# Unread identity products on TensorE ahead of eleven waits of a two-block transformer kernel

## What is computed

```
x = first_block(x, c, ctx, c_ctx, ...)    # attention layer, then a Hyena long-convolution layer, then rms_norm
x = second_block(x, c_2, ...)             # even layer: conv + stick-breaking attention, then a mixture of experts
                                          # odd layer: gated linear recurrence, then a mixture of experts
# every layer: h = rms_norm(x) * (1 + scale) + shift ; x = x + gate * mixer(h)
# shift, scale, gate = silu(c) @ mod_w + mod_b
# attention layer: 8 grouped-query heads and 8 latent heads over 256 context + 1024 own tokens
# experts: 16 experts, 4 groups, two experts for each token, silu(x@w1) * (x@w3) @ w2
```

## Time and profile before

| | us |
|---|---|
| median of 3 runs | 4669.76 |
| lowest and highest | 4667.46 and 4686.14 |
| the profiled execution's own time | 4669.6 |
| span of the profile (first to last instruction) | 4667.8 |

### The profile page before, as it was taken

One profiled execution on the slowest core, in us unless ns is written; L12 is line 12 of the kernel. 1 busy time (PEld: TensorE's weight loads), 2 busy tenths in 40 slices (PEclk: granted clock), 3 DMA queues, 4 the chain that ended last, 5 costly groups with the idle time before them and its releaser, 6 DMA issues. The chain is left out here.

```text
span 4667.8 us, 76042 instructions
## 1 busy us (share of the span) xinstructions
PE 4083.4 (87%) x28639; PEld 2076.3 (44%) x28639; DVE 2024.0 (43%) x3133; ACT 1044.1 (22%) x2136; POOL 266.1 (6%) x382
## 2 busy tenths in 40 slices
PE   4799799998999998999599978868999599949995
PEld 1445366564444446878344435432333244413331
DVE  1233588773222207999447737441111334321112
ACT  0122355441111112222020336211010244100000
POOL 0100000000000000111100000000000200000001
PEclk7899799999999989999799989989999799969997
DMA  8122433334445410111520030246963611376767
GB/s 329 29 71 66 97 77 86 79 84 170 173 183 221 147 64 12 55 56 55 181 95 26 38 118 28 91 154 259 362 261 126 194 36 50 104 312 250 273 232 269
DMA packets 254230, 643.61 MB, mean 138 GB/s; under 512 B 53434, under 2 KB 132372, under 8 KB 218176
## 3 DMA queue, kind: packets, MB, share of 16 engines
q1 hardware_dynamic: 218312, 524.26, 32.2%
q0 software_dynamic: 19424, 94.01, 5.6%
q10 hardware_dynamic: 16280, 22.27, 1.3%
HBM read 1325.95 MB, written 113.53 MB: 308 GB/s over the span
## 5 line engine op out<-in xcount | busy, mean ns | idle before, releaser
L1085 PE MATMUL att_acc<-att_kT,att_qT 96*128 96x512 f32 (+3 forms) x768 | 305.9, 583 | 35.9 <-DMA att_kT<-scratch_KT 19.7
L1741 PE MATMUL hyp_acc<-hy_hT,hyp_early_weights 128*128 128x512 f32 x768 | 335.9, 596 | 0.0
L3641 PE MATMUL blocks_h<-moe_w,blocks_xT 128*32 128x512 f32 x2560 | 294.2, 612 | 19.0 <-DMA moe_w<-in_ex_w 19.0
L3641 PE MATMUL blocks_h<-od_hT,blocks_xT 128*32 128x512 f32 x1280 | 288.2, 604 | 21.3 <-DMA moe_w1b<-in_ex_w 16.2
L3641 PE MATMUL blocks_h<-moe_w1b,blocks_xT 128*32 128x512 f32 x1280 | 288.2, 604 | 0.0
L3663 PE MATMUL blocks_acc<-moe_w,blocks_hidT 128*32 128x512 f32 x2560 | 284.6, 597 | 3.4 <-DMA moe_w<-in_ex_w 2.1
L1004 DVE TENSOR_REDUCE att_part_max<-att_acc 128x1 f32<-128x512 f32 (+1 forms) x384 | 214.6, 586 | 98.3 <-PE att_acc L1085 98.3
L2396 PE MATMUL evp_acc<-ev_hT,evp_early_weights 128*128 128x512 f32 x512 | 225.7, 602 | 7.6 <-DVE evp_qkT L2537 5.6
L1741 PEld LDWEIGHTS hyp_acc<-hy_hT,hyp_early_weights 128*128 128x128 f32 x768 | 145.2, 192 | 174.1 <-issue 174.0
L1085 PEld LDWEIGHTS att_acc<-att_kT,att_qT 64*128 64x128 f32 (+1 forms) x768 | 130.0, 198 | 127.3 <-issue 82.9
L3641 PEld LDWEIGHTS blocks_h<-od_hT,blocks_xT 128*32 128x32 f32 x1280 | 76.7, 112 | 216.1 <-issue 212.2
(11 more groups left out here) (555 smaller groups left out, 6528.9 us busy)
## 6 DMA issues: line engine op xcount, KB each, us to landing
moe_w<-in_ex_w SPq DMA_DIRECT2D x640, 1024.0 KB
od_hT<-in_ex_w SPq DMA_DIRECT2D x168, 1024.0 KB
moe_w1b<-in_ex_w SPq DMA_DIRECT2D x168, 1024.0 KB
hyp_m_weights<-in_mod_w POOLq DMA_DIRECT2D x6, 8192.0 KB, 24.9
mod_weights<-in_ada_w SPq DMA_DIRECT2D x12, 2048.0 KB, 20.7
att_v<-scratch_V SPq DMA_DIRECT2D x64, 320.0 KB, 5.7
scratch_y_rows<-blocks_x ACTq DMA_DIRECT2D x40, 512.0 KB, 7.7
hyp_early_weights<-in_hy_w_in SPq DMA_DIRECT2D x8, 2048.0 KB, 27.2
```

What stands on the lines that cost most here:

```text
L1085: nc.tensor.matmul(scores(j, c), qT[e, s, cols], kT[e, s, CHUNKS[c]], start=True, stop=True).then_inc(scored[c], 1)
L1741: mm = nc.tensor.matmul(acc[:, m % 2, half * NC:(half + 1) * NC], weights[:, ws, kt, c:c + P], hT[:, kt, half * NC:(half + 1) * NC], start ...
L3641: mm = nc.tensor.matmul(out[mine, :], xT[:, kt, mine], w[l][:, kt, :], start=(kt == 0), stop=(kt == KT - 1))
```

## The change

`keep_busy` issues `4 * us` matmuls that multiply the identity with itself, start and stop set, into a part of PSUM which the stage's first real product overwrites. They stand in TensorE's list ahead of a wait. No semaphore is raised or waited for by them. `stage_modulations` gets `ident` as a new argument. Nothing is removed, and no other engine's list changes.

```diff
+def keep_busy(nc, out, ident, us):
+    for _ in range(4 * us):
+        nc.tensor.matmul(out, ident[:, 0:out.shape[0]], ident[:, 0:out.shape[1]], start=True, stop=True)
...
# stage_modulations
+                keep_busy(nc, acc[:, 0, 0:P], ident, 10)
                 pe.wait_ge(svec_ready, signals(1))
# attention_project (ctx and lat)
+                keep_busy(nc, acc[:, 0, 0:P], ident, 5)
                 pe.wait_ge(cols_in, signals(16 * 3))
# stage_attention
+                keep_busy(nc, acc[:, 0:P], ident, 14)
                 pe.wait_ge(stacked, signals(1))
# project_out (ao, ho and eo), first in TensorE's list
+                keep_busy(nc, acc[:, 0, 0:P], ident, 8)
# stage_stick_breaking
+                keep_busy(nc, scores[:, 0, 0:P], ident, 9)
                 pe.wait_ge(barred_ready, signals(1))
# stage_recurrence
+                keep_busy(nc, px[:, 0, 0:P], ident, 6)
                 blocks(pe, front, back)
# moe_blocks (twice), first in TensorE's list
+                keep_busy(nc, acc[:, 0, 0:P], ident, 8)
                 pe.wait_ge(tables_in, signals(16 * 3))
...
                 nc.tensor.matmul(owner_row, owner_col, ident[:, 0:PLACES], start=True, stop=True).then_inc(owner_turned, 1)
+                keep_busy(nc, acc[:, 0, 0:P], ident, 6)
                 pe.wait_ge(located, signals(1))
...
                 def first():
+                    keep_busy(nc, acc[:, 0, 0:P], ident, 7)
                     rows(0, 0)
# moe_combine, with a norm
+                    keep_busy(nc, h_turn[:, 0, 0, :], ident, 5)
                     pe.wait_ge(cols_in, signals(16 * 3))
                     nc.tensor.transpose(col_turn[:, :], col_rows[:, :], ident[0:3 * KT, 0:3 * KT]).then_inc(cols_turned, 1)
+                    keep_busy(nc, h_turn[:, 0, 0, :], ident, 9)
                     for t in range(TT):
```

More of the change, by code:

```diff
@@ L209, in load_rows, with stage_modulations @@
         sp.dma_start(early.col_rows[n * KT:(n + 1) * KT, :], v.rearrange("(kt p) -> kt p", p=P)).then_inc(early.cols_in, 16)
-def stage_modulations(nc, d, svec, early):
+def stage_modulations(nc, d, ident, svec, early):
     S, Q = 2, MODS_AT_ONCE
@@ L3972, in program @@
             early = Projection(nc, outer)
-            stage_modulations(nc, d, svec, early)
+            stage_modulations(nc, d, ident, svec, early)
             stage_attention_project(nc, d, ident, early)
```

## The result

| | before | after |
|---|---|---|
| median of 12 runs, us | 4670.68 | 4691.57 |
| lowest and highest | 4664.37, 4686.14 | 4686.49, 4699.32 |
| ratio, 95% interval | | 1.0046, 1.0038 to 1.0054 |
| span of the profile | 4667.8 | 4691.6 |

The change makes the kernel 20.9 us slower, 0.46%. The forecast was 4676, +6 us; the time lies in the range given, near its upper end. So the sign was right and 15 of the 21 us were missing.

The account below looks back on a forecast made before the run. TensorE was taken to bound most stages, with gains only in dense work at the low clock just behind a wait. The places' terms summed to +6.1 us on 4669.6, about 4676, range 4656 to 4694.

Parts of the forecast that it names:

- `project_out`: Stages `ao`, `ho`, `eo`: 32 products each overshoot their room; net +0.7, 0 and +1.6 us.
- Prices: Every fill: a product takes 0.22 us at the high clock, 0.44 at the low one.
- The low part of a fill: Start of every fill: the clock stays low for 3 to 6 us, taken as 4, before it rises.
- the first rival: All fills: identity products don't raise the clock, each lasts 0.44 us; about +80 us, 4750; 7 in 100.
- rivals 1 and 2: All fills: products don't raise the clock (4750, 7 in 100), or cost 0.38 us each (4700, 5 in 100).
- Attention: Attention: 56 products overshoot by 7.5 us, faster first scores return part, the raised clock is soon lost; net +3 us.
- The third rival: Clock holds through the attention's scores and gaps in `ctx`, `lat`, `ao`: 4662, or 4650; 8 in 100.
- `lat`: Stage `lat`: room 2.8 us, fill 6.4, part returned by faster transposes and projection; net +2 us, bounds +1 and +3.6.
- `ctx`: Stage `ctx`: room 2.0 us, fill 6.4, 3.4 returned by the high clock; net +1 us, bounds -0.7 and +4.4.
- recurrence: Recurrence: fill overshoots by 0.4 us, the 32 passes behind it regain 1.6; net -1.2 us, bounds -1.5 and +1.
- Stick-breaking: Stick-breaking attention: overshoot 4.2 us, hidden by values arriving late and faster scores; 0, bounds -0.5 and +3 us.
- The rule: Whole kernel: penalty is throttled length times one minus granted share, 327 us; the prediction held only 27 us at most buyable.

Follow-up runs that it names:

- e7: The kernel before with 112 added products in the attention alone, instead of 56: 4699.43 us, ratio 1.0068 to before.
- e4: The kernel before with the change's 56 products in the attention alone: 4674.42 us, ratio 1.0010 to before.
- e6: The kernel before with 20 products ahead of the attention's first wait and 4 behind the scores of each of its first four tiles: 4660.12 us.
- e9: The kernel before with e6's attention products, 12 in `eo` behind the two increments and 24 in the recurrence: 4660.16 us, ratio 0.9978.
- e5: The kernel before with 20 products in the attention, 12 in `eo` behind the two increments, 24 in the recurrence, none elsewhere: 4663.79 us.
- e1: The changed kernel with the 32 products in `project_out` moved behind TensorE's two increments: 4679.28 us, ratio 1.0021 to before.
- the third pair: Two executions of e10, attention 2.0 us apart: 4663.99 us (median of its runs) and 4665.98 us (the single second execution).
- e10: The kernel before with 4 products behind the scores of each of the attention's first four tiles, no fill ahead: 4663.99 us, ratio 0.9987.

## Why the prediction was right, and where it was not

The time lies in the range because the range was 38 us wide, and the place that made most of the loss was priced at almost nothing. That the time came out inside is in part luck. The mechanism was right for the products themselves and wrong for what stood behind them in `project_out`.

**Prices: right.** A product was put at 0.22 us; e7 against e4 gives 0.2225. The low part of a fill was put at 3 to 6 us: 5.6 in the attention, and the fills' durations fit (7.25 for 20 products forecast at 6.4, 9.28 for 32 at 9.0, 7.04 for 24 at 7.3, 15.44 and 14.52 for 56 at 14.3). Identity products raise the clock, so the first rival was wrong. The row held against it was weaker than the prediction made of it: the 16 transposes at `eo` last 3.87 us and the clock was low for 6.0, so matmuls filled the rest. The 0.12 for slower is rivals 1 and 2 alone, with nothing in it for a tail of the forecast.

**Attention: right mechanism, size within its bounds.** Start at the block's start, clock low and then high, first eight scores in 2.84 us, clock lost in the first tiles: all as written. +3 was forecast, 3.8 and 5.0 us were measured by adding and removing the fill. The third rival's clock that holds by itself didn't come; e6, e9 and e5 show how far filled gaps help.

**`lat`: right; `ctx` and recurrence: not to be told from chance.** `lat` +1 to +2.7 for +2, with L633 now released by TensorE. `ctx` came out at -2.1 to +0.2 for the +1, but a kernel without products there had -2.4. The recurrence's 32 passes took 13.90 us for the 14 forecast; the stage itself lay between -2.4 and +2.5 for the -1.2.

**`project_out`: the step that failed.** The prediction costed the products there as an overshoot only: "an overshoot of this size ends in the 7.33 us in which TensorE waited" (`ho`), "the third tile's gate product waits for a transfer until 1085.37 in any case" (`ao`). Both took the arrival of the transfers as fixed. They aren't: the list of TensorE begins with two increments that release the sync queue's loads, and the products stood ahead of them. The later gates moved with the loads, in `ao` the third one by 11.0 us (from 1085.37 to 1096.34) against a stage start that was 5.3 later. Forecast +0.7, 0 and +1.6; measured +5.7, +3.6 and +3.6. With the increments first (e1) the same products cost -0.2, +0.1 and +2.9, a sum of 2.8 for the forecast 2.3: close as a sum, with `ao` 0.9 us below and `eo` 1.3 above their terms, for the code that I had in mind, and wrong for the code in the diff. The place ahead of a queue's release was 12.3 of the missing 15 us.

**Stick-breaking: under-sized.** 0 was forecast with +3 as the upper bound, -0.2 or +3.4 came. Of the 3.4 in the changed kernel 1.3 are there 17 us behind the block's start, the rest comes later, with the low stretches; whether the products in `ho` place these is open. The long convolution's +3.7 in the profiled run is chance and belongs to no step. Expert stages and combine moved by 1 to 2 us in both directions, within their bounds.

**The rule.** The prediction weighed the Trainium skill's penalty, TensorE: Matmul & The Clock Gate, section Terms, against what stands directly behind a release. The runs bear the second out: 118 us of low clock fewer would be an estimated 59 us by that rule, and the kernel became slower. It does fit two pairs of executions in the attention's later tiles (10.6 us more at the low clock, 5.4 us longer; 7.5 and 4.0), and not the third pair.

## What to carry to other kernels

Before anything is put at the head of an engine's list, look what stands behind it that others wait for, increments above all: they take no time in the profile and can release a whole stage's transfers. Size filling work by the time from the block's start to the release, not by the idle time shown, and let it end just short of it: 12 products behind the increments earned 3.0 us where 32 behind them cost 2.9 and 32 ahead of them 3.6. Where a raised clock is lost again in a stretch short of work, a few passes in its gaps (1.2 us per tile in the attention) were worth more than a long fill ahead of it (4660.12 in e6 against 4674.42 in e4).

## What the runs showed of the hardware

- The two increments behind 64 passes took effect ahead of the passes' end: SP issued 1.9 us before the fill's end, as the profile models it, in all three stages (1071.19 against 1073.11 in `ao`). So TensorE's instruction stream runs ahead of its array there.
- Whether passes over 64 rows keep a raised clock depends on what stands between them: 0.50 from 535.4 in the changed kernel and from 524.0 in e5, 1.00 throughout in e6, lost and regained within 7 us in e9. In e10 the clock rose from the low level behind the third group of the same gap products.
- Executions of one program differ by where the clock is low in the same work: 51 against 40 us of low clock in the attention's later tiles of the changed kernel. The attention's stage spread over 7 us among kernels with the same code in it. In the stick-breaking attention the low stretches lay at the same distances within 0.1 us in four profiles of three kernels. The Trainium skill, in TensorE: Matmul & The Clock Gate, section Part 1: The HAM clock gate, says that the monitor behind the clock isn't aligned with the kernel's start, so that the turning points vary from run to run. The two profiles of the changed kernel agree at the attention, where the clock rose 5.7 and 3.9 us behind the block's start; the four in the stick-breaking attention show no such spread.
